# Norms: VectorE adds the squares of two row blocks before TensorE sums them, and the remainder of the next weight tile moves from ahead of the norm to behind it

## The reference, cut to what matters

```python
def rms_norm(x, g):
    xf = x.astype(jnp.float32)
    y = xf * lax.rsqrt(jnp.mean(xf * xf, axis=-1, keepdims=True) + EPS)
    ...

# first block, for each of 2 layers
x = x + 0.5 * swiglu(rms_norm(x, ffn1_norm[l]), ffn1_w_gu[l], ffn1_w_down[l])
h = rms_norm(x, mix_norm[l])
...                                   # x = x + merged @ w_mix_out[l]
x = x + cross_attention(rms_norm(x, xattn_norm[l]), rms_norm(mem, mem_norm[l]), ...)
x = x + 0.5 * swiglu(rms_norm(x, ffn2_norm[l]), ffn2_w_gu[l], ffn2_w_down[l])
# then
x = rms_norm(x, final_norm)
# second block, for each of 2 layers; mod = silu(c) @ w_ada[l] + b_ada[l], split in nine
h = modulate(rmsnorm(x, norm_g[layer, 0]), sh1, sc1)
x = x + 0.5 * g1 * swiglu_2(h, ...)
h = modulate(rmsnorm(x, norm_g[layer, 1]), sh2, sc2)
...                                   # x = x + g2 * (o @ w_out[layer])
h = modulate(rmsnorm(x, norm_g[layer, 2]), sh3, sc3)
x = x + 0.5 * g3 * swiglu_2(h, ...)
```

## Time and profile before

| | |
|---|---|
| median of 3 runs | 3065.47 us (3065.07 to 3066.64) |
| the profiled execution's own time | 3064.59 us |
| its span | 3062.4 us |
| PE busy | 2942.2 us (96%) |
| DVE busy | 2088.6 us (68%) |
| ACT busy | 1314.9 us (43%) |
| mean granted PE clock | 0.974 |

### The profile page before, as it was taken

One profiled execution on the slowest core, in us unless ns is written; L12 is line 12 of the kernel. 1 busy time (PEld: TensorE's weight loads), 2 busy tenths in 40 slices (PEclk: granted clock), 3 DMA queues, 4 the chain that ended last, 5 costly groups with the idle time before them and its releaser, 6 DMA issues.

```text
span 3062.4 us, 52325 instructions
## 1 busy us (share of the span) xinstructions
PE 2942.2 (96%) x23184; PEld 2868.1 (94%) x23192; DVE 2088.6 (68%) x2644; ACT 1314.9 (43%) x1300; POOL 205.2 (7%) x163
## 2 busy tenths in 40 slices
PE   8999999999999999999999999999799999997999
PEld 8999998999999999999999999988599999885999
DVE  7777867556776668857657767767667766776554
ACT  5344545444333345544444343344543433445332
POOL 0000420000000001500000000011000000110000
PEclk9999999999999999999999989999899999998999
DMA  7654433435666644433446646633056566431354
GB/s 271 241 201 174 143 124 136 167 138 207 238 216 237 244 179 166 138 127 135 167 159 223 256 168 234 249 136 138 14 215 243 203 250 241 170 112 40 138 180 150
DMA packets 78464, 549.07 MB, mean 179 GB/s; under 512 B 8480, under 2 KB 11936, under 8 KB 12320
## 3 DMA queue, kind: packets, MB, share of 16 engines
q1 hardware_dynamic: 67152, 464.99, 42.4%
q0 software_dynamic: 11088, 80.75, 6.5%
HBM read 544.65 MB, written 1.05 MB: 178 GB/s over the span
## 4 chain that ended last, share of the span: by engine, by line
PE 80%; DVE 12%; ACT 4%; issue 2%; POOL 2%; DMA 0%; DVEq 0%; POOLq 0%; SPq 0%; ACTq 0%
PE ps L301 72%; DVE ring_lo L295 3%; ACT w_hi L288 2%; PE ps L373 1%; PE ps L747 1%; PE ps L497 1%; POOL qk L1492 1%; DVE hk L1201 1%; POOL rope_a L1488 1%; PE ps L877 0%; DVE e L400 0%; DVE e L1259 0%; DVE e L1258 0%; DVE a_hg L1279 0%; PE ps L1610 0%
## 5 line engine op out<-in xcount | busy, mean ns | idle before, releaser
L295 DVE TENSOR_TENSOR ring_lo<-ring,w_hi 128x2048 fp32r<-128x2048 f32 x438 | 1009.0, 2306 | 646.4 <-ACT w_hi L288 641.7
L301 PE MATMUL ps<-h_hi,w_hi 128*128 128x256 f32 x4688 | 1350.9, 288 | 39.9 <-DVE h_lo L2004 17.2
L301 PE MATMUL ps<-h_lo,w_hi 128*128 128x256 f32 x4688 | 1336.0, 285 | 0.0
L301 PE MATMUL ps<-h_hi,ring_lo 128*128 128x256 f32 x4688 | 1335.0, 285 | 0.0
L288 ACT ACTIVATE w_hi<-ring 128x2048 fp32r<-128x2048 f32 x438 | 837.1, 1911 | 727.6 <-PE ps L301 663.1
L301 PEld LDWEIGHTS ps<-h_hi,w_hi 128*128 128x128 f32 x4688 | 909.8, 194 | 52.0 <-issue 44.8
L301 PEld LDWEIGHTS ps<-h_lo,w_hi 128*128 128x128 f32 x4688 | 909.9, 194 | 4.6 <-issue 4.0
L301 PEld LDWEIGHTS ps<-h_hi,ring_lo 128*128 128x128 f32 x4688 | 909.5, 194 | 0.0
L301 PE MATMUL ps<-g_hi,w_hi 128*128 128x256 f32 x1408 | 398.5, 283 | 0.0
L301 PE MATMUL ps<-g_lo,w_hi 128*128 128x256 f32 x1408 | 398.5, 283 | 0.0
L301 PE MATMUL ps<-g_hi,ring_lo 128*128 128x256 f32 x1408 | 398.5, 283 | 0.0
(11 more groups left out here) (307 smaller groups left out, 3130.0 us busy)
## 6 DMA issues: line engine op xcount, KB each, us to landing
ring<-stream SPq DMA_DIRECT2D x438, 1024.0 KB, 4.8
e<-ada POOLq DMA_DIRECT2D x77, 1024.0 KB, 5.1
x<-x_t SPq DMA_DIRECT2D x4, 256.0 KB, 4.9
mem<-mem_t SPq DMA_DIRECT2D x1, 1024.0 KB, 10.3
out_t<-x SPq DMA_DIRECT2D x4, 256.0 KB, 2.1
con_sb<-con SPq DMA_DIRECT2D x1, 896.0 KB, 14.9
con_sb<-con SPq DMA_DIRECT2D x1, 640.0 KB, 5.9
hq<-lmask SPq DMA_DIRECT2D x1, 512.0 KB, 15.6
```

The lines of the kernel that those rows point to most:

```text
L295: nc.vector.tensor_tensor(ring_lo[:, p % RING, :], ring[:, p % RING, :], w_hi[:, p % HIGHS, :].bitcast(F32), ALU.subtract).then_inc(S.w_lo ...
L301: mm = nc.tensor.matmul(out, a, b, start=start and n == 0, stop=stop and n == 2, skip_group_check=group)
```

## The change

Three edits.

1. A new function `paired` on DVE adds the squares of row block 2b+1 to those of row block 2b, in place in `e_buf[0]`, as soon as ACT's squares of b are there, and raises a new semaphore `sq_paired`. `norm_pe` now has four matmuls instead of eight, and waits for `sq_paired`.
2. `paired(b)` is called inside `residual`, one bank late: after x of bank b and before its `gains` comes `paired(b - 1)`, and after the loop `paired(3)`. At the start of the program, ahead of X, and in the first norm of the second block it is called after each `gains` instead.
3. Where a `low` stood between the residual and `norm_dve` (FFN_A of layer 1, MIX, FFN_C, Z, the final norm), it now stands behind the norm. At the start of the program and ahead of X it stays.

```diff
         def norm_pe(pe, n, sq):
-            for k in range(KD):
-                if k % 2 == 0:
-                    pe.wait_ge(S.sq_ready, nth(S.sq_ready, 4 * n + k // 2 + 1))
-                mm = nc.tensor.matmul(ps[:, 0, 0:T], ones, sq[:, k, :], start=(k == 0), stop=(k == KD - 1))
+            for b in range(4):
+                pe.wait_ge(S.sq_paired, nth(S.sq_paired, 4 * n + b + 1))
+                mm = nc.tensor.matmul(ps[:, 0, 0:T], ones, sq[:, 2 * b, :], start=(b == 0), stop=(b == 3))
             mm.then_inc(S.ss_ready, 1)
+
+        def paired(dve, n, b):
+
+            dve.wait_ge(S.sq_ready, nth(S.sq_ready, 4 * n + b + 1))
+            nc.vector.tensor_tensor(e_buf[0][:, 2 * b, :], e_buf[0][:, 2 * b, :], e_buf[0][:, 2 * b + 1, :],
+                                    ALU.add).then_inc(S.sq_paired, 1)
...
-        def residual(dve, ready, bank, scale, then=None):
+        def residual(dve, ready, bank, scale, then=None, n=None):
...
                     ins.then_inc(S.x_ready, 1)
+                if n is not None and b >= 1:
+                    paired(dve, n, b - 1)
                 if then:
                     then(b)
+            if n is not None:
+                paired(dve, n, 3)
...
                 for b in range(4):
                     dve.wait_ge(x_loaded[b], 16)
-                    ins = gains(dve, None, v_now[:, V1_FFN1:V1_FFN1 + KD], b)
-                chain(ins)
+                    gains(dve, None, v_now[:, V1_FFN1:V1_FFN1 + KD], b)
+                    paired(dve, 0, b)
                 low(dve, FFN_A)
                 norm_dve(dve, chain, 0)
...
             residual(dve, ffn_banks(dve, FFN_A, 0), 4, 0.5,
-                     lambda b: gains(dve, 4, v_now[:, V1_MIX:V1_MIX + KD], b))
+                     lambda b: gains(dve, 4, v_now[:, V1_MIX:V1_MIX + KD], b), 1)
+            norm_dve(dve, chain, 1)
             low(dve, MIX - 2 + HIGHS)
-            norm_dve(dve, chain, 1)
             low(dve, MIX - 1 + HIGHS)
...
         def final_dve(dve, chain):
-            low(dve, DEPTH * TILES_1 - 2 + HIGHS)
             rstd_dve(dve, chain, 0)
...
                 for b in range(4):
-                    ins = gains(dve, 0, parts[1], b)
-                chain(ins)
+                    gains(dve, 0, parts[1], b)
+                    paired(dve, 0, b)
                 dve.wait_ge(S.con_next, 16)
-            else:
-                low(dve, FFN_C - 2 + HIGHS)
             norm_dve(dve, chain, 0, parts[0])
+            low(dve, FFN_C - 2 + HIGHS)
             low(dve, FFN_C - 1 + HIGHS)
```

More of the change, by code:

```diff
@@ L111 @@
-    yb_used=4, ya_used=4, merged=2, mem_ready=1, ada_step=176, ada_done=22, ada_summed=2, mod_ready=2, log_done=4,
-    h_scaled=16, h_hi_ready=16, down_done=6,
+    sq_paired=16, pool_chain=12, merged_hi=2, mem_hi_ready=1, att_hi_ready=8, silu_done=24, hidden_step=44,
+    prod_done=24, x_ready=16, sq_ready=16, ss_ready=4, rstd_ready=4, h_ready=16, evac_done=54, forget_ready=1,
+    log_ready=1, cumsum_ready=1, decay_arg=8, decay_exp=8, e_ready=8, level_done=18, level_used=18, a_zeroed=1,
+    rot_done=12, rot_scaled=12, rope_done=12, o_done=2, o_copied=2, o_ss=1, o_var=1, o_rstd=1, o_ready=1,
@@ L113 @@
+    scores_done=8, scores_read=12, max_ready=8, exp_ready=8, probs_ready=8, pt_done=8, pt_ready=8, pv_done=8,
+    att_ready=8, yb_used=4, ya_used=4, merged=2, mem_ready=1, ada_step=176, ada_done=22, ada_summed=2,
+    mod_ready=2, log_done=4, h_scaled=16, h_hi_ready=16, down_done=6,
 )
 FINAL_TOTAL = dict(
-    x_ready=4, sq_ready=4, ss_ready=1, rstd_ready=1, log_done=1,
+    x_ready=4, sq_ready=4, ss_ready=1, rstd_ready=1, log_done=1, sq_paired=4,
 )
 TWO_TOTAL = dict(
-    pool_chain=7, silu_done=24, hidden_step=44, prod_done=24, x_ready=12, sq_ready=12, ss_ready=3, rstd_ready=3,
@@ L119 @@
[L119 to L123, removed]
@@ L124 @@
-    wi_ready=2,
+    sq_paired=12, pool_chain=7, silu_done=24, hidden_step=44, prod_done=24, x_ready=12, sq_ready=12, ss_ready=3,
+    rstd_ready=3, h_ready=12, evac_done=15, rot_done=7, rot_scaled=7, rope_done=7, o_done=8, o_sq=4, o_ss=4,
+    o_var=4, o_rstd=4, o_ready=4, scores_done=8, scores_read=8, max_ready=8, exp_ready=8, probs_ready=8,
+    pt_done=8, pt_ready=8, pv_done=8, ada_step=176, ada_done=22, ada_summed=2, mod_ready=2, head_sq=4, head_ss=4,
+    head_var=4, head_rs=4, head_ready=4, ki_ready=1, logit_done=6, relu_ready=6, relu_used=6, z_done=8,
@@ L125 @@
+    zm_ready=8, soft_ready=8, l_ready=8, log_done=3, h_scaled=12, h_hi_ready=12, down_done=6, cum_done=8,
+    arg_ready=8, a_ready=8, wi_ready=2,
 )
@@ L1173, in one_dve @@
             else:
+                norm_dve(dve, chain, 0)
                 low(dve, FFN_A - 2 + HIGHS)
-                norm_dve(dve, chain, 0)
                 low(dve, FFN_A - 1 + HIGHS)
@@ L1421, in one_dve @@
                 gains(dve, 8, v_now[:, V1_X:V1_X + KD], b)
+                paired(dve, 2, b)
             low(dve, M_KV1 + HIGHS)
@@ L1453, in x_last @@
                     low(dve, X_O + b + HIGHS)
-            residual(dve, one_by_one(dve, X_O), 4, 1.0, x_last)
+            residual(dve, one_by_one(dve, X_O), 4, 1.0, x_last, 3)
             norm_dve(dve, chain, 3)
@@ L1469, in one_dve @@
             ffn_dve(dve, l, 0, FFN_B, 1, between=ahead)
-            residual(dve, ffn_banks(dve, FFN_B, 1), 4, 0.5, first_gains)
+            residual(dve, ffn_banks(dve, FFN_B, 1), 4, 0.5, first_gains, 4)
         def one_pool(pool, l):
@@ L1867, in two_dve @@
             ffn_dve(dve, l, DEPTH, FFN_C, 0)
-            residual(dve, ffn_banks(dve, FFN_C, 0), 4, parts[2], lambda b: gains(dve, 4, parts[4], b))
+            residual(dve, ffn_banks(dve, FFN_C, 0), 4, parts[2], lambda b: gains(dve, 4, parts[4], b), 1)
+            norm_dve(dve, chain, 1, parts[3])
             low(dve, Z_QI - 2 + HIGHS)
-            norm_dve(dve, chain, 1, parts[3])
             low(dve, Z_QI - 1 + HIGHS)
@@ L2023, in z_last @@
                     low(dve, Z_O + b + HIGHS)
-            residual(dve, one_by_one(dve, Z_O), 0, parts[5], z_last)
+            residual(dve, one_by_one(dve, Z_O), 0, parts[5], z_last, 2)
             norm_dve(dve, chain, 2, parts[6])
@@ L2036, in two_dve @@
             ffn_dve(dve, l, DEPTH, FFN_D, 1, products=l < DEPTH - 1, between=ahead)
-            residual(dve, ffn_banks(dve, FFN_D, 1), 4, parts[8], first_gains)
+            residual(dve, ffn_banks(dve, FFN_D, 1), 4, parts[8], first_gains, 3 if l < DEPTH - 1 else None)
         def two_pool(pool, l):
```

7 lines of the change are left out of this document (1 added, 6 removed).

## The result

| | before | changed kernel |
|---|---|---|
| median of 9 runs each, same chip | 3065.2 us (3063.5 to 3066.6) | 3075.2 us (3069.7 to 3077.6) |
| ratio | | 1.003, 95% interval 1.0021 to 1.0039 |
| profiled execution, its span | 3064.6, 3062.4 | 3077.6, 3075.8 |
| mean granted PE clock | 0.974 | 0.968 |
| time at half clock (records of the clock, summed) | 159.9 us | 200.2 us |

The account below looks back on a forecast made before the run. Four fifths of the chain run through PE, so a norm costs what it holds up PE. Terms without the clock -0.9, clock +7.9, sum +7.0 on the median 3065.5: 3072.5 us, range 3063 to 3078.

Parts of the forecast that it names:

- The log: In the norms, log bound by the table load: 0.48 earlier in MIX and FFN_A of layer 1, 0.2 later in Z.
- The costs of an addition on DVE: `paired` on DVE takes 0.42, costing 0.34 in the queue or 0.24 where it fills the gap between x and gains.
- The clock term, +7.9: In seven `ada_pe` after the start, the thinned sum makes PE's clock fall earlier: 1.1 each, +7.9, bounds 0 and +12.
- The rival that short waits don't matter: In `ada_pe`, short waits don't matter to the clock: -0.9, 3064.6 (3062 to 3067), not slower; chance 0.21.
- The start, +3.9: At program start, the sum waits for gains and `ada_pe` queues behind it: bounds +1.3 and +6, +3.9 taken.
- the -2.8 for FFN_B and FFN_D: Four norms of FFN_B and FFN_D: log earlier by 0.79 and 0.59, counted whole as PE idles until DVE's first remainder.
- the -1.1 for the final norm and FFN_C of layer 0: Final norm -0.8 as FFN_B; in the norm after it, additions pace the sum, ending some 0.3 nearer: -1.1 together.
- the moved remainders cost nothing: `low` behind the norm delays only the second and third tiles' remainders, hidden; without that cover each costs up to 2.3.
- The rival of DVE becoming the bound: In the residuals, additions cost 0.42 to 0.47, last x 0.4 later in six norms: +2.4, 3075 to 3078; chance 0.10.
- The baseline: The sum of +7.0 was added to the median of before, 3065.5, not to the profiled execution of 3064.6.

Follow-up runs that it names:

- experiment 3: Changed kernel with two extra matmuls filling each norm's sum: 3067.3 us written into the sum's own bank, 3068.5 us on constants into another bank.
- experiment 2: Kernel before with only the start changed (four additions ahead of the first tile's `low`, four matmuls): 3071.2 us, ratio 1.0014.
- experiment 1: Changed kernel with its first norm, at the start, as before (eight matmuls straight on ACT's squares): 3069.6 us, ratio 1.0016.
- experiment 6: Kernel before with additions and four matmuls only in FFN_B, FFN_D and the final norm, the last with its remainder behind it: 3067.2 us, ratio 1.0003.
- 5: Kernel before with only the remainders (`low`) moved behind the norm, eight matmuls, no additions: 3064.3 us, ratio 0.9997.
- 4: Changed kernel with the remainders (`low`) back ahead of the norms, except FFN_D and X, where there is none: 3075.7 us, ratio 1.003.

## Why the prediction was right

**The log.** It starts 0.02 or less behind the table load in every norm where that was forecast. The gains came out at 0.58 (MIX, FFN_A; forecast 0.48), 0.79 (FFN_B and final; 0.79) and 0.60 (FFN_D; 0.59), X at 0, Z and FFN_C of layer 1 at 0.16 late (0.2). There, in the changed kernel, the two x of the last bank and the load of the table behind them:

```profile
2028.81 0.87 DVE L579 SCALAR_TENSOR_TENSOR x<-ps,mod,x 128x256 f32<-128x256 f32 x2
...
2030.36 1.28 ACT L351 ACT_TABLE_LOAD   x1
2031.67 0.47 ACT L353 ACTIVATE rstd<-ps,eps 128x256 f32<-128x256 f32 x1
```

The sum began at 2027.84, so this x stands at +0.97; before it stood at +0.56: 0.4 late, forecast 0.5. The costs of an addition on DVE, forecast as 0.34 in the queue and 0.24 in the gap, are 0.33 and 0.20 in the MIX norm. With the smaller one x of the last bank is 0.21 late there instead of 0.30, which is the 0.1 that the log gained beyond its forecast.

**The clock term, +7.9.** Measured as 9.5 more on the seven `ada_pe` in the trace, and as 7 to 8 of the whole time by filling the sum. The mechanism is shown by experiment 3: the same DVE work, the same log, only PE's sum denser. The rival that short waits don't matter has fallen. No gap within a sum was longer than 0.95 us, and yet the six stretches without a long wait ahead of them went from 34.7 to 41.8. The Trainium skill, "TensorE: Matmul & The Clock Gate", section "HAM oscillation — how this bites in real kernels", asks for no long idle gap of PE; by these rows that alone doesn't keep the clock here, and before the change, with no gap in the sum at all, it had fallen in three of these six already. The size was less of a reading than the mechanism: 7.9 came from half of a span between two bounds and a feedback taken in part (seven times 1.1 is 7.7, not 7.9), and norm by norm the seven changed by -0.2 to +2.5. That the sum came out is in part luck.

**The start, +3.9.** 2.9 in the changed kernel's trace, 5.7 in that of experiment 2, and 5.6 and 6.2 by the medians of 1 and 2. `var` came at 17.7 (forecast 18.1), the tile at 24.16 and 27.43 (bounds 23.4 and 27.6). The mechanism, `ada_pe` behind a PE that stood idle, was right; I took the middle (of 1.3 and 6 that would be 3.65, not 3.9), and by the medians the upper end is nearer.

**Terms that were mis-sized.** First, the -2.8 for FFN_B and FFN_D. I wrote "PE idles until DVE's first remainder, so this counts whole". It does, but the thin sum costs clock there too, in the tiles behind: in the two profiled executions +0.4, +0.2, -0.3 and -0.3, together 0. Averaged over the profiles in the table of experiment 6 it is -1.5, about half of the term. I had given the clock only to norms with `ada_pe`. Second, the -1.1 for the final norm and FFN_C of layer 0: the two logs came earlier (3.84 against 6.35 in the second), but `ada_pe` then ran at half clock in full, 9.39. With the clock that part is +1.4 in this pair, where the terms made it 0. It isn't sized by that: the same part took 39.0 in experiment 1, with four matmuls, and 41.5 and 37.1 in 2 and 5, with eight. The median missed by 2.7; terms read from one profile don't add up closer than that.

**What was hidden.** That the moved remainders cost nothing is shown by 4 and 5 together; in 4 the trace shows `ada_pe` as the cover. The rival of DVE becoming the bound (+2.4 for x in six norms) has fallen: x was 0.4 late in Z by the additions' plain cost, and no norm's log came later than forecast.

**The baseline.** I added the sum to the median of before (3065.5); the nine runs beside the changed kernel gave 3065.2.

## What to carry to other kernels

Taking matmuls away from PE in front of a stretch of tiny ones can cost more than they took: count, ahead of every such stretch, what keeps the clock there, and read the granted clock behind each change of PE's density, also in the tiles that follow. Where PE has to wait for another engine anyway, give it work there: first its own (independent small matmuls in the gaps of a chained sum), then matmuls on constants into a free bank. With that the kernel with these additions went from 0.3% slower to 0.4% faster.

## What the runs showed of the hardware

- A sum of four matmuls with waits of 0.45 and 0.16 us between them, in place of eight without a wait, brought more half clock into the stretch behind: in FFN_A of layer 1 `ada_pe` went from 6.89 at 0.70 to 8.11 at 0.59, with the sum filled to 5.00 at 0.98.
- The granted clock fell inside `ada_pe`, 44 records back to back without a pause of PE: its mean was 0.68 to 0.77 in four of seven stretches before. The same records took 4.97 at 1.00 and 9.39 at 0.50.
- The same instructions get other clocks in other executions. At the start, with the same sum at 13.2 and 13.3, `ada_pe` took 6.29 once and 9.38 once. The nine runs of the changed kernel spread over 8 us (3069.7 to 3077.6), the nine of before over 3, and the sets of 25 to 30 of before over 5.5 to 6. A single profile places a clock loss, it doesn't size it; that took the sums over seven stretches and medians of 7 or more runs.
- In the changed kernel the log starts 0.01 to 0.02 behind a table load of 1.28, in every norm where the load is what ends last.
